# Rounded token-major products with falling column patterns in a two-block transformer kernel

## The reference

```python
proj = h @ w_in[l]                       # first block, 2048 x 5656
x = x + rms_norm(mix @ w_out[l], ...)    # 2048 x 2048
u = causal_dwconv(h @ w_up[l], ...)      # 2048 x 11264
y = (gelu(gate) * up) @ w_down[l]        # 5632 x 2048
proj = h @ w_in                          # second block, 2048 x 5376
mixed @ w_out                            # 2048 x 2048
u = relu(h @ w_up); y = (u * u) @ w_down # 2048 x 8192, 8192 x 2048
```

## Time and profile before

| | |
|---|---|
| Time, median of 3 runs | 2238.05 us (2237.18 to 2239.73) |
| The profiled execution | span 2235.6 us, the only time that it gives |
| TensorE busy | 2215.5 us, 99% of the span, 12721 matmuls |
| TensorE weight loads | 1891.4 us, 85% |
| VectorE, ScalarE, GpSimd busy | 1416.2 us (63%), 1118.0 us (50%), 65.7 us (3%) |
| HBM | read 414.85 MB, written 2.49 MB: 187 GB/s over the span |
| Weight DMAs (queue 1) | 58.3% of 16 engines |
| Mean granted TensorE clock | 0.999 |

### The profile page before, as it was taken

One profiled execution on the slowest core, in us unless ns is written; L12 is line 12 of the kernel. 1 busy time (PEld: TensorE's weight loads), 2 busy tenths in 40 slices (PEclk: granted clock), 3 DMA queues, 4 the chain that ended last, 5 costly groups with the idle time before them and its releaser, 6 DMA issues.

```text
span 2235.6 us, 34152 instructions
## 1 busy us (share of the span) xinstructions
PE 2215.5 (99%) x12721; PEld 1891.4 (85%) x12721; DVE 1416.2 (63%) x1827; ACT 1118.0 (50%) x1567; POOL 65.7 (3%) x95
## 2 busy tenths in 40 slices
PE   8999999999999999999999999999999999999998
PEld 7888888888888888888888888888888888888887
DVE  6466685677776447777566786657666444666545
ACT  5454464555555445555454554545444444444443
POOL 5100000000000000000000000000000000000000
PEclk9999999999999999999999999999999999999999
DMA  9954455566566666666657455566666666666663
GB/s 291 317 180 133 132 167 181 162 190 205 178 201 195 190 194 189 187 188 200 209 147 206 142 162 160 180 195 167 196 191 193 191 196 190 191 192 188 214 192 112
DMA packets 321663, 418.84 MB, mean 187 GB/s; under 512 B 13566, under 2 KB 233048, under 8 KB 320788
## 3 DMA queue, kind: packets, MB, share of 16 engines
q1 hardware_dynamic: 316548, 398.81, 58.3%
q0 software_dynamic: 4720, 16.49, 2.5%
q10 hardware_dynamic: 288, 2.10, 0.3%
HBM read 414.85 MB, written 2.49 MB: 187 GB/s over the span
## 4 chain that ended last, share of the span: by engine, by line
PE 95%; DVE 2%; DMA 1%; issue 1%; ACT 1%; POOL 0%; POOLq 0%; DVEq 0%; SPq 0%; ACTq 0%
PE PS L2024 25%; PE PS L2028 13%; PE PS L1912 10%; PE PS L1911 10%; PE PS L1913 10%; PE PS L2097 5%; PE PS L2368 3%; PE PS L2100 2%; PE PS L2113 2%; PE PS L2115 2%; PE PS L2114 2%; PE PS L2371 2%; PE PS L2381 1%; PE PS L2383 1%; PE PS L2382 1%
## 5 line engine op out<-in xcount | busy, mean ns | idle before, releaser
L2024 PE MATMUL PS<-actu,whi 128*128 128x512 f32 x2432 | 755.6, 392 | 0.0
L2028 PEld LDWEIGHTS PS<-actu,wlo 128*128 128x128 f32 x2432 | 457.1, 188 | 99.9
L1226 DVE TENSOR_TENSOR wlo<-stage,whi 128x1024 fp32r<-128x1024 f32 x296 | 360.4, 1223 | 216.5 <-ACT whi L790 216.2
L1198 DVE TENSOR_TENSOR wlo<-stage,whi 128x1024 fp32r<-128x1024 f32 x245 | 298.9, 1225 | 301.2 <-ACT whi L732 301.2
L2028 PE MATMUL PS<-actu,wlo 128*128 128x256 f32 x2432 | 480.0, 279 | 0.0
L790 ACT ACTIVATE whi<-stage 128x1024 fp32r<-128x1024 f32 x296 | 311.4, 1057 | 304.9 <-PE PS L2028 291.6
L732 ACT ACTIVATE whi<-stage 128x1024 fp32r<-128x1024 f32 x245 | 258.7, 1060 | 344.6 <-PE PS L1913 321.4
L2024 PEld LDWEIGHTS PS<-actu,whi 128*128 128x128 f32 x2432 | 368.4, 188 | 0.6 <-issue 0.4
L1913 PE MATMUL PS<-whi,gT 128*128 128x512 f32 x864 | 336.4, 389 | 0.0
L1912 PE MATMUL PS<-wlo,gT 128*128 128x512 f32 x864 | 336.4, 389 | 0.0
L1911 PE MATMUL PS<-whi,gT 128*128 128x512 f32 x864 | 336.4, 389 | 0.0
(11 more groups left out here) (338 smaller groups left out, 2482.4 us busy)
## 6 DMA issues: line engine op xcount, KB each, us to landing
stage<-in_w_up SPq DMA_DIRECT2D x304, 512.0 KB, 3.9
stage<-in_w_down SPq DMA_DIRECT2D x216, 512.0 KB, 4.2
stage<-in_w_in SPq DMA_DIRECT2D x160, 512.0 KB, 3.8
stage<-in_w_out SPq DMA_DIRECT2D x64, 512.0 KB, 4.2
stage<-in_w_in SPq DMA_DIRECT2D x16, 256.0 KB, 4.0
DQK<-in_cmp_k_w POOLq DMA_DIRECT2D x8, 512.0 KB, 6.6
DQK<-in_cmp_v_w POOLq DMA_DIRECT2D x8, 512.0 KB, 6.3
stage<-in_w_in SPq DMA_DIRECT2D x8, 280.0 KB, 8.3
```

What stands on the lines that cost most here:

```text
L1198: nc.vector.tensor_tensor(wlo[:, s % SPLITS, 0:wd], stage[:, s % STAGES, 0:wd], whi[:, s % SPLITS, 0:wd].bitcast(F32), ALU.subtract).then_ ...
L1226: nc.vector.tensor_tensor(wlo[:, j % SPLITS, :], stage[:, j, :], whi[:, j % SPLITS, :].bitcast(F32), ALU.subtract).then_inc(ev("lo_done"), 1)
L2024: nc.tensor.matmul(o, whi[:, j % SPLITS, at], actu[:, k, :], start=k == 0, stop=False)
L2028: last = nc.tensor.matmul(o[:, S:2 * S], wlo[:, j % SPLITS, at], actu[:, k, 0:S], start=False, stop=k == KC - 1)
```

## The change

In the nine token-major matmuls of rounded operands, the moving operand is read from its last column to its first, and the output is written from its last column to its first. The stationary operand, the flags, the waits and the signals are as before, and so is every other matmul.

```diff
+            def falling(ap):
+
+                return ap[:, ::-1]
+
             def chunk(o, lhs, k, s, c, t, ends):
...
-                nc.tensor.matmul(o, ah, h, start=k == 0, stop=False)
-                nc.tensor.matmul(o, ah, l, start=False, stop=False)
-                return nc.tensor.matmul(o, al, h, start=False, stop=ends and c == TC - 1)
+                nc.tensor.matmul(falling(o), ah, falling(h), start=k == 0, stop=False)
+                nc.tensor.matmul(falling(o), ah, falling(l), start=False, stop=False)
+                return nc.tensor.matmul(falling(o), al, falling(h), start=False, stop=ends and c == TC - 1)
...
-                        nc.tensor.matmul(o, ah, h, start=at_k == 0, stop=False)
-                        nc.tensor.matmul(o, ah, l, start=False, stop=False)
-                        last = nc.tensor.matmul(o, al, h, start=False, stop=at_k == KC - 1)
+                        nc.tensor.matmul(falling(o), ah, falling(h), start=at_k == 0, stop=False)
+                        nc.tensor.matmul(falling(o), ah, falling(l), start=False, stop=False)
+                        last = nc.tensor.matmul(falling(o), al, falling(h), start=False, stop=at_k == KC - 1)
```

## The result

The kernel after takes 2263.31 us (median of 4 runs, 2262.13 to 2264.17) where the kernel before takes 2237.61 us in the same comparison (4 runs, 2236.86 to 2239.73): 25.7 us more, a ratio of 1.0114 with a 95% interval of 1.0100 to 1.0129. It is slower by 1.1%, well clear of the interval; the forecast was no change. The value lies inside the range of 2211 to 2292 us, on the side of the rival "slower by little".

A forecast was written before the change was run, and what follows sets the result against it. TensorE's start-to-start pace was taken to bound the kernel; reading downward, writing downward and the fixed part each added 0 to the median of 2238.05 us, giving 2238.0 us, with a range of 2211 to 2292 us.

The forecast's parts named there:

- no change: Whole kernel: the token-major cadence stays at 0.2267 us, total 2238.0 us, within 0.2%; chance 0.64.
- slower by little: Rival, each touched matmul's head or tail: falling setup adds half the fixed part, 27 us (2265 us), doubling 2292 us; chance 0.09.
- What bounds the kernel: TensorE, busy 99% of the span: what a token-major matmul takes from start to start goes into the total one for one.
- the count: Touched token-major lines: 3936 matmuls of 512 columns, 96 of 280 and 192 of 256, together 927 us, 41% of the span.
- Reading the weights downward: Moving operand of the token-major matmuls: same words fetched, neighbour after neighbour, so 0.4176 ns a column stays, cost 0.
- The fixed 0.0129 us: Part of each touched matmul's time beyond its columns, whatever its width: 54 us in all, taken to change by 0.
- Writing the bank downward: Output of the token-major matmuls: same 512 words of one bank, no column touched sooner than before, cost 0.
- all products of a bank fall alike: Token-major outputs: all three products of a chunk and all chunks of a bank fall, so no column is revisited sooner.
- The bounds that I set for both halves together: Reading and writing in the touched matmuls: from 0.4176 ns a column, unchanged, up to two cycles for a column.
- the forecast's own test: Touched matmuls: a cost per matmul would move 512-, 280- and 256-column ones all by the same few ns.
- Slower by much: Rival, token-major fetch or store: falling costs cycles per column, 873 us more (3111 us), 109 us at one in eight; chance 0.18.
- Faster: Rival, touched matmuls: the fixed part shrinks, half of it gives 27 us (2211 us), all of it 2184 us; chance 0.09.

The follow-up runs named there:

- words_falling: Kernel before, with both operands of the nine token-major lines rising in groups of 4 words and falling inside each group: 2237.78 us, ratio 1.0003.
- micro2: Kernel without both blocks, only series of 40 rounded matmuls varying the stationary operand's columns, step and start: at 32 stationary columns 231 ns rising, 233 falling.

## Why the prediction was wrong

- **What bounds the kernel** was right: every ns of TensorE's cadence went into the total, 24.7 us of busy time into 24.7 us of span, and ScalarE only waited longer. So was the count: 3936 matmuls of 512 columns carry the whole difference.
- **"Reading the weights downward ... I take no change: the same words are fetched, neighbour after neighbour"** is the step that failed. The order of words within 16 bytes is indeed free (`words_falling`), but that of the pieces is not: 6.6 ns a matmul. The Trainium skill ("SBUF — State Buffer", section "Door 1: The DMA port swizzle") says that the SBUF has lines of 16 bytes, that accesses in a row to one line run at full bandwidth and that each crossing to a new line has a price. On that unit the runs agree, with words reversed inside groups of 4 free and inside groups of 8 not. But a full reversal takes the four words of each line in a row as well, so the page alone wouldn't give the 6.6 ns. The step took the walk by itself and never against the weight load beside it, and that load's place moves the cadence of a rising walk too (226.7 to 233.3 ns).
- **"The fixed 0.0129 us ... I take 0, since ... the weight load ... and the order are unchanged"** failed with it. The 13 ns aren't a fixed restart: with two-byte operands 216 ns are left of 226.7, and with the stationary operand 8 words further on the same rising series takes 233. Nor do they stand whatever the width: beyond a column a cycle, rising matmuls take 13 ns at 512, 384 and 256 columns but 58 at 128, and falling ones 20, 18 and 12 at the first three.
- **Writing the bank downward** at nothing was right (ratio 1.0005), and so was the argument that all products of a bank fall alike. The bounds that I set for both halves together (column for column up to double) were far too wide for what happened: 233.3 against 226.7 ns is 3%.
- **The rivals.** "Slower by little" gave 2265 us, within 2 us of the result, but by another mechanism: it had the cost at each matmul's head and alike at every width, and the forecast's own test for it fails, since 256 columns got 1.7 ns faster. So it is luck that the time lies inside the range. "Slower by much" was near in kind, as the order of groups of words does count where they are read, and far off in size: the smallest price that it named, one cycle in eight columns, is 64 cycles a matmul, and 16 were measured at 512 columns. "Faster" is seen only at 256 columns, in 192 matmuls, 0.3 us, and even there it isn't the direction as such: with 96 stationary columns a rising series of 256 takes 116.2 ns and a falling one 120.0 (`micro2`, lines 101, 103). A chance of 0.64 for no change rested on the lack of a row about falling patterns; that the two operands share something couldn't be read from one cadence, but the two feature-major products could have hinted at it: the same four matmuls take 690 ns in the feed-forward parts and 697 in the input products of the trace of before.
- **A reading**: TensorE's row of slices has an 8 in the last slice as well as in the first; nothing in the forecast hangs on it.

## What to carry to other kernels

When TensorE's matmuls follow each other without a gap, the cadence of four-byte operands hangs on where stationary and moving operand begin against each other, by a few per cent. Here token-major products were fastest with both beginning at the same place modulo 64 words, and moving a small tensor in front of the weights cost 14 us. Keep moving operands rising in pieces of 16 bytes; output patterns may fall. Check in the kernel itself, or with a series of some 40 matmuls that has the kernel's own addresses and order of operands: series that shared only the relative place gave 233.3 and 228.9 ns at one place, and one and the same series 233.3 and 226.7.

## What the runs showed of the hardware

- Two-byte operands of 512 columns start every 215.8 ns, rounded four-byte ones every 226.7 at best. The Trainium skill ("TensorE: Matmul & The Clock Gate", section "Part 2: What happens when you issue a matmul") says that the moving operand and the weight load have independent ports and don't take bandwidth from each other. Nothing in the two-byte series speaks against that; in the four-byte ones the two aren't independent in time, as the start of the stationary operand alone moves the cadence from 226.7 to 233.3 ns.
- Most settled cadences of 512 columns are 226.7 or 233.3 ns, 16 cycles apart at 2.4 GHz; a few falling series have 236.7 or 240.0, and some rising ones values between 228.9 and 235.0. After a change of pattern some matmuls pass until a series settles (the first four steps of line 129 of `micro2` are 243, 231, 235 and 234 ns).
- At 256 columns and 64 stationary ones a rising series took 113.3 ns for 120.0, while at 512 the smaller load cost more, not less (230.0). What the two operands share, why only rising walks find a good place, and why one place can settle at two cadences, stays open: the runs show where the cadence changes, not the mechanism behind it.
